# Two residual blocks on one core: the spatial gating unit computes v's columns before u's, and its layer norm and heads' mixing are issued among the large products

## What is computed

```python
def sgu_mixer(h, w_in, ln_g, ln_b, w_s, b_s, w_out):
    z = jax.nn.gelu(h @ w_in, approximate=False)
    u, v = jnp.split(z, 2, axis=-1)
    v = layernorm(v, ln_g, ln_b)
    v = v.reshape(B_, nc, SGU_CHUNK, SGU_HEADS, SGU_HEAD_DIM)
    ws = jnp.where(mask[None], w_s, 0)
    mixed = jnp.einsum('hts,bnshc->bnthc', ws, v) + b_s.T[None, None, :, :, None]
    gated = u * mixed.reshape(B_, S_, SGU_WIDTH)
    return gated @ w_out
```

## Time and profile before

| | |
|---|---|
| median of 3 runs | 2000.14 us |
| lowest, highest | 1999.51, 2003.49 us |
| the profiled execution, its time | 2002.35 us |
| its span in the profile | 2000.9 us |
| PE busy | 1825.2 us, 91% |
| DVE busy | 1052.0 us, 53% |
| ACT busy | 645.0 us, 32% |
| granted TensorE clock, mean over the span | 0.941 |

### The profile page before, as it was taken

One profiled execution on the slowest core, in us unless ns is written; L12 is line 12 of the kernel. 1 busy time (PEld: TensorE's weight loads), 2 busy tenths in 40 slices (PEclk: granted clock), 3 DMA queues, 4 the chain that ended last, 5 costly groups with the idle time before them and its releaser, 6 DMA issues.

```text
span 2000.9 us, 21459 instructions
## 1 busy us (share of the span) xinstructions
PE 1825.2 (91%) x8828; PEld 1473.2 (74%) x8828; DVE 1052.0 (53%) x1336; ACT 645.0 (32%) x796; POOL 82.5 (4%) x87
## 2 busy tenths in 40 slices
PE   4659999999896899999999989976599999999997
PEld 2238888888685688888886868855388888888885
DVE  4874675477426544234356574444565642456533
ACT  2123312322322243123244523332244431344412
POOL 2400010000000000000000101000000000000000
PEclk8769999999897899999998989987699999999997
DMA  9713474366230232323322240002123323232321
GB/s 356 275 64 105 143 236 151 102 209 222 74 105 9 76 105 87 104 88 102 105 90 69 85 100 4 4 1 66 40 85 105 100 90 105 84 105 91 100 84 42
DMA packets 124000, 208.55 MB, mean 104 GB/s; under 512 B 13965, under 2 KB 48421, under 8 KB 123904
## 3 DMA queue, kind: packets, MB, share of 16 engines
q1 hardware_dynamic: 115424, 174.94, 26.7%
q0 software_dynamic: 7808, 29.43, 4.4%
q10 hardware_dynamic: 672, 2.82, 0.4%
HBM read 204.01 MB, written 4.73 MB: 104 GB/s over the span
## 4 chain that ended last, share of the span: by engine, by line
PE 85%; DVE 10%; ACT 2%; DMA 1%; issue 1%; SPq 1%; DVEq 0%; ACTq 0%
PE bank L531 73%; DVE ada_acc L1643 2%; DMA ada_ring<-in_ada_w 1%; PE bank L878 1%; PE bank L547 1%; PE bank L861 1%; PE bank L841 1%; SPq L476 1%; PE bank L542 1%; DVE gT L1969 1%; DVE outer L1967 0%; PE bank L923 0%; PE bank L673 0%; PE bank L902 0%; PE bank L950 0%
## 5 line engine op out<-in xcount | busy, mean ns | idle before, releaser
L1568 DVE TENSOR_TENSOR w_lo<-raw,w_hi 128x2048 fp32r<-128x2048 f32 x138 | 316.2, 2292 | 533.0 <-ACT w_hi L1140 533.0
L1140 ACT ACTIVATE w_hi<-raw 128x2048 fp32r<-128x2048 f32 x138 | 263.8, 1912 | 632.7 <-PE bank L531 609.8
L531 PE MATMUL bank<-u_hi,w_hi 128*128 128x512 f32 x768 | 300.6, 391 | 0.8 <-DVE conv L2225 0.8
L531 PE MATMUL bank<-h_hi,w_hi 128*128 128x512 f32 x736 | 292.8, 398 | 7.9 <-DVE h_lo L1615 7.7
L531 PE MATMUL bank<-u_hi,w_lo 128*128 128x512 f32 x768 | 299.1, 389 | 0.0
L531 PE MATMUL bank<-u_lo,w_hi 128*128 128x512 f32 x768 | 298.9, 389 | 0.0
L531 PE MATMUL bank<-h_lo,w_hi 128*128 128x512 f32 x736 | 289.4, 393 | 0.0
L531 PE MATMUL bank<-h_hi,w_lo 128*128 128x512 f32 x736 | 289.2, 393 | 0.0
L531 PE MATMUL bank<-f_hi,w_hi 128*128 128x512 f32 x512 | 200.4, 391 | 2.4 <-DVE f_lo L1618 2.4
L531 PE MATMUL bank<-f_lo,w_hi 128*128 128x512 f32 x512 | 199.9, 391 | 0.0
L531 PE MATMUL bank<-f_hi,w_lo 128*128 128x512 f32 x512 | 199.8, 390 | 0.0
(11 more groups left out here) (351 smaller groups left out, 2040.3 us busy)
## 6 DMA issues: line engine op xcount, KB each, us to landing
raw<-in_mlp_w SPq DMA_DIRECT2D x128, 512.0 KB, 4.6
raw<-in_w_ffn_up SPq DMA_DIRECT2D x64, 512.0 KB, 4.4
ada_ring<-in_ada_w POOLq DMA_DIRECT2D x24, 1024.0 KB, 5.8
ada_ring<-in_ada_w SPq DMA_DIRECT2D x9, 2048.0 KB, 13.9
raw<-in_w_ffn_down SPq DMA_DIRECT2D x32, 512.0 KB, 4.4
raw<-in_w_in SPq DMA_DIRECT2D x20, 512.0 KB, 4.4
raw<-in_sgu_w_in SPq DMA_DIRECT2D x16, 512.0 KB, 4.9
x_rows<-in_ada_w SPq DMA_DIRECT2D x3, 2048.0 KB, 11.8
```

The source lines that it names most:

```text
L531: mm = te.matmul(bank[:, n], a, b, start=first and k == 0 and j == 0, stop=last and k == 3 and j == 2)
L1140: se.activation(m.ring(s)[0], m.raw[:, slot], ACT.Copy).then_inc(sem("hi_made"), 1)
L1568: ve.tensor_tensor(lo, m.raw[:, slot], hi.bitcast(F32), ALU.subtract).then_inc(sem("lo_made"), 1)
```

## The change

The same products and the same small operations are issued in another order.

- The weight slabs of `sgu_in` come in the order of column groups 2, 3, 0, 1. Groups 0 and 1 now make v, groups 2 and 3 make u.
- PE issues the turning and the bias spread after slab 34, the column sums inside slab 35 (after its second tile), heads 0 to 3 after the four tiles of slab 38, heads 4 and 5 after slab 39, and heads 6 and 7 after the first two tiles of slab 40. `sgu_out`'s first slab is no longer in k-outer order.
- ACT copies the bias during group 1, takes the root between slab 37's rounding and slab 38's, and rounds heads 0 to 3 ahead of slab 40's rounding, 4 and 5 ahead of slab 41's, 6 and 7 behind it.
- DVE masks between the `w_lo` of slabs 35 and 36, folds the bias, takes statistics and normalises between those of 36 and 37, and gates heads 0 to 3 behind slab 39's, 4 and 5 behind slab 40's, 6 and 7 behind slab 41's.

The core of the diff:

```diff
-    out = mlp(0) + linear(t["sgu_w_in"], 2, range(4)) + linear(t["sgu_w_out"], 2, range(2)) + mlp(1)
+    out = mlp(0) + linear(t["sgu_w_in"], 2, (2, 3, 0, 1)) + linear(t["sgu_w_out"], 2, range(2)) + mlp(1)
...
+    def spatial_weights(k, n):
+        if (k, n) == (0, 3):
+            te.wait_ge(sem("ws_in"), 32)
+            te.wait_ge(sem("scaled"), 8 * NORMED[NORM_MIX1] + 8)
+            for hh in range(DT):
+                mm = te.transpose(bank[:, 4 + hh // 4, P * (hh % 4):P * (hh % 4) + P], m.ws[:, hh], ident)
...
+        elif (k, n) == (1, 1):
+            te.wait_ge(sem("ws_masked"), MILESTONE["ws_masked"])
+            te.wait_ge(sem("bs_copied"), MILESTONE["bs_copied"])
...
+    def first_heads(k, n):
+        if k == 0:
+            mix_head(n)
+
+    def last_heads(k, n):
+        if k == 0 and n < 2:
+            mix_head(6 + n)
...
-    two_slabs("sgu_out", 2, m.g_hi, m.g_lo, gated, k_outer=True)
+    two_slabs("sgu_in", 0, m.h_hi, m.h_lo, lambda k: normed(NORM_MIX1, k), weights_stationary=False, k_outer=True)
+    two_slabs("sgu_in", 1, m.h_hi, m.h_lo, weights_stationary=False, beside=spatial_weights)
+    two_slabs("sgu_in", 2, m.h_hi, m.h_lo)
+    two_slabs("sgu_in", 3, m.h_hi, m.h_lo, beside=first_heads)
+    mix_head(4)
+    mix_head(5)
+    two_slabs("sgu_out", 0, m.g_hi, m.g_lo, gated, beside=last_heads)
+    two_slabs("sgu_out", 1, m.g_hi, m.g_lo)
...
         split_to(s + 1)
+        if g == 1:
+            se.wait_ge(sem("bs_spread"), MILESTONE["bs_spread"])
+            se.activation(m.bs[:, :], bank[:, 6:8].rearrange("p b n -> p (b n)"), ACT.Copy).then_inc(sem("bs_copied"), 1)
+        if g == 2:
+            se.wait_ge(sem("v_stats"), 4)
+            se.activation(m.mv[:, :, 1:2], m.mv[:, :, 1:2], ACT.Sqrt, bias=m.eps[:, 1:2]).then_inc(sem("v_rooted"), 1)
+        if g == 3:
+            gated_hi(range(4))
         split_to(s + 2)
...
+    gated_hi(range(4, 6))
+    split_to(SLABS["sgu_out"] + 1)
+    gated_hi(range(6, 8))
...
+    first = SLABS["sgu_in"]
+    split_to(first + 3)
     ve.wait_ge(sem("ws_turned"), MILESTONE["ws_turned"])
...
+    split_to(first + 4)
...
+    v_stats()
+    v_normed()
     ve.wait_ge(own.sem, bs_ready)
...
+    split_to(first + 7)
+    gate(range(4))
+    split_to(first + 8)
+    gate(range(4, 6))
+    split_to(first + 9)
+    gate(range(6, 8))
```

More of the change, by code:

```diff
@@ L685, in tensor_program @@
     norm_spread(NORM_MIX1)
[L688 to L716, removed]
+    def two_slabs(name, g, hi, lo, before_k=None, weights_stationary=True, k_outer=False, beside=None):
+        group, s = GROUPS[name] + g, SLABS[name] + 2 * g
+        for k in range(2):
+            def before_n(n):
+                emptied(group - 1, n)
+            def wait_k(kk):
+                before_k(4 * k + kk)
+            def after_n(n):
+                if beside:
+                    beside(k, n)
+            slab(s + k, group, hi[:, 4 * k:4 * k + 4], lo[:, 4 * k:4 * k + 4], k == 0, k == 1,
+                 wait_k if before_k else None, before_n, weights_stationary, k_outer and k == 0, after_n)
+            after_n(3)
@@ new lines, in spatial_weights @@
+    def spatial_weights(k, n):
[4 more added lines that the diff above has]
+                mm = te.transpose(bank[:, 4 + hh // 4, P * (hh % 4):P * (hh % 4) + P], m.ws[:, hh], ident)
+            mm.then_inc(sem("ws_turned"), 1)
+            for q in range(2):
+                mm = te.matmul(bank[:, 6 + q], ones[0:1, :], m.bs_row[0:1, 512 * q:512 * q + 512], start=True, stop=True)
+            mm.then_inc(sem("bs_spread"), 1)
+        elif (k, n) == (1, 1):
+            te.wait_ge(sem("ws_masked"), MILESTONE["ws_masked"])
+            te.wait_ge(sem("bs_copied"), MILESTONE["bs_copied"])
+            for q in range(2):
+                mm = te.matmul(bank[:, 6 + q], ones[:, :], m.wsT[:, 4 * q:4 * q + 4].rearrange("p h t -> p (h t)"), start=True, stop=True)
+            mm.then_inc(sem("ws_summed"), 1)
@@ L717, in tensor_program, with mix_head @@
+    def mix_head(hh):
         if hh >= 2:
@@ L1265, in scalar_program, with gated_hi @@
     normalise_hi(NORM_MIX1, m.h_hi, lambda k: m.modv(1, 0, k))
+    def gated_hi(heads):
+        for hh in heads:
+            se.wait_ge(sem("gated"), hh + 1)
+            se.activation(m.g_hi[:, hh], m.u[:, hh], ACT.Copy).then_inc(sem("gated_hi"), 1)
     for g in range(4):
@@ L1271, in scalar_program @@
             full(s + 1, group, n)
-            place = m.u[:, 4 * g + n] if g < 2 else m.v[:, n, 512 * (g - 2):512 * (g - 2) + 512]
+            place = m.v[:, n, 512 * g:512 * g + 512] if g < 2 else m.u[:, 4 * (g - 2) + n]
             se.activation(place, bank[:, n], ACT.Gelu).then_inc(sem("act_emptied"), 1)
[L1274 to L1280, removed]
+    gated_hi(range(4, 6))
+    split_to(SLABS["sgu_out"] + 1)
+    gated_hi(range(6, 8))
     for g in range(2):
@@ L1811, in vector_program, with v_stats, v_normed, gate @@
     normalise_lo(NORM_MIX1, m.xT, m.h_lo, m.h_hi, lambda k: m.gain[:, 16 + k:17 + k], lambda k: m.modv(1, 0, k))
-    for g in range(4):
-        split_to(SLABS["sgu_in"] + 2 * g + 2)
+    def v_stats():
+        for n in range(4):
+            for q in range(2):
+                emptied(GROUPS["sgu_in"] + q, n)
+                st = own.on(ve.bn_stats(m.stats[:, n, q], m.v[:, n, 512 * q:512 * q + 512]))
+            ve.wait_ge(own.sem, st)
+            ve.bn_aggr(m.mv[:, n], m.stats[:, n]).then_inc(sem("v_stats"), 1)
+    def v_normed():
+        ve.wait_ge(sem("v_rooted"), MILESTONE["v_rooted"])
+        ve.wait_ge(sem("v_stats"), 4)
+        n = own.on(ve.reciprocal(m.mv[:, :, 1:2], m.mv[:, :, 1:2]))
+        ve.wait_ge(own.sem, n)
+        for n in range(4):
+            ve.tensor_scalar(m.v[:, n], m.v[:, n], m.mv[:, n, 0:1], m.mv[:, n, 1:2], ALU.subtract, ALU.mult).then_inc(sem("v_normed"), 1)
+    def gate(heads):
+        for hh in heads:
+            ve.wait_ge(sem("heads_full"), hh + 1)
+            ve.scalar_tensor_tensor(out=m.tmp[:, hh % 2].rearrange("p (n t) -> p n t", n=4),
+                                    in0=bank[:, 4 + hh % 2].rearrange("p (n t) -> p n t", n=4), scalar=m.col("sgu_ln_g", hh),
+                                    in1=m.bs[:, P * hh:P * hh + P].unsqueeze(1).broadcast_to([P, 4, P]),
+                                    op0=ALU.mult, op1=ALU.add).then_inc(sem("heads_mixed"), 1)
+            ve.wait_ge(sem("heads_mixed"), hh + 1)
+            emptied(GROUPS["sgu_in"] + 2 + hh // 4, hh % 4)
+            ve.tensor_tensor(m.u[:, hh], m.u[:, hh], m.tmp[:, hh % 2], ALU.mult).then_inc(sem("gated"), 1)
+            ve.wait_ge(sem("gated"), hh + 1)
+            ve.wait_ge(sem("gated_hi"), hh + 1)
+            ve.tensor_tensor(m.g_lo[:, hh], m.u[:, hh], m.g_hi[:, hh].bitcast(F32), ALU.subtract).then_inc(sem("gated_lo"), 1)
+    first = SLABS["sgu_in"]
+    split_to(first + 3)
     ve.wait_ge(sem("ws_turned"), MILESTONE["ws_turned"])
@@ L1823, in vector_program @@
     bs_ready = n
[L1824 to L1835, removed]
-    ve.wait_ge(own.sem, bs_ready)
[L1837 to L1847, removed]
+    v_stats()
+    v_normed()
+    ve.wait_ge(own.sem, bs_ready)
+    split_to(first + 7)
[4 more added lines that the diff above has]
+    gate(range(6, 8))
     for g in range(2):
```

## The result

| | before | changed |
|---|---|---|
| median of 5 runs | 1999.58 us | 1977.61 us |
| lowest, highest | 1999.46, 2003.49 | 1975.86, 1982.51 |
| the profiled execution | 2002.35 | 1977.91 |
| its span | 2000.9 | 1976.5 |

The ratio of changed to before is 0.9887, with a 95% interval of 0.9872 to 0.9901. The kernel is 22.0 us faster by the medians and 24.4 us by the spans of the two profiled executions. The forecast was 1975.8 us, 24.3 us faster; the measured median lies 1.8 us above it, within the range of 1973 to 1982.5.

A forecast was written before the change was run, and what follows sets the result against it. PE bounds the kernel, busy 91% of the span; the SGU stretch offers 37.71 us, less 13.4 us of small matmuls among the products, a gain of 24.3: 2000.14 - 24.3 = 1975.8 us, range 1973 to 1982.5.

The forecast's parts named there:

- What was to win: Between sgu_in and sgu_out: 36.64 us of PE mostly waiting plus 1.07 us of slow start, 37.71 us.
- sums: Column sums on PE, 4 pieces moved among the products: 1.92 us at full clock.
- heads: Eight heads' matmuls on PE among the products: 8 x 0.97 = 7.76 us.
- changes: 18 changes between kinds of matmul on PE: 0.05 us each, 0.9 in all, with ends of 0 and 2.2.
- rival 2: Heads wait for one another through DVE's strict queue; slab 41 comes 11 us late, 1984 to 1992 us; chance 0.06.
- the 0.12 outside the range: Chance of a time outside 1973 to 1982.5 us, which the prediction gave to the two rarer rivals.
- At slab 37 I had 1.1 us of cover: Behind the layer norm: slab ready at 9.8 us after slab 35's end, due at 10.9.
- At slab 41 I had 0.7: Behind the gates: head 7 gated at 41.7 us after slab 38's start, wanted at 42.4; the thinnest place.
- Rival 1: Rounding or gates come late at slab 37, 41 or both, paid once: 1977 to 1983 us, middle 1979; chance 0.18.
- a rare rival that costs slabs or nothing: Short matmuls among products, slabs 38 to 40, lower PE's clock, 10.88 us per slab; chance 0.02 slower, 0.02 partly.
- no wait is met only at the end of the stage: Denies the rival that one such wait brings the serial stretch back, time as before within 4 us; chance 0.02.
- The slower case: From 2.3 slabs at half clock, of six from 38 to 43, the change is slower; all six give 2041; chance 0.02.

The follow-up runs named there:

- the delay: Two unneeded DVE additions in the changed kernel, ahead of the normalising (slab 37: 1979.08 us) or of the gates of heads 6 and 7 (slab 41: 1983.75 us).
- the order alone: The changed kernel with v's columns still computed first, but all small work issued behind the last slab as before: 2001.14 us, ratio 0.9998 to before.
- The doubled heads: The changed kernel with each head's four matmuls issued twice in the same place, the second time over the first result: 1986.71 us, ratio 0.9928 to before.

## Why the prediction was right

**The terms.** What was to win, 37.71 us, was read correctly from the one execution of before. The small matmuls in the stream cost 0.87 + 1.91 + 1.72 + 8 x 0.89 = 11.6 us by the chain, and 0.45 us for all the changes between them (110.0 less nine slabs of 10.88 and the 11.6), in all 12.1; I had said 13.4. Three terms were a little too large: sums 1.92 for 1.72, heads 7.76 for 7.12 (the weight loads of a head span 0.97 us, but the next product starts 0.89 us after the head's first matmul), changes 0.9 for 0.45. With the measured terms, 37.7 - 12.1 = 25.6 us, which is the stretch's gain. Two slips in the text of the prediction moved nothing: rival 2 has PE wait 0.6 us for each head in one clause and 1.4 in the next, and the 0.12 outside the range belongs to three rivals, not two.

**The covers.** At slab 37 I had 1.1 us of cover; the trace has 1.4, and the delay found 1.25. At slab 41 I had 0.7; the trace has 0.8, and the delay found 0.65. Both experiments found the edge where it was said to be. Rival 1 did not happen, but it would need only a microsecond to.

**The table load.** The row says 1.28 us and the root begins 0.01 us behind it, so a switch of set takes 1.29 us here, not the 2.66 that the Trainium skill gives in "ScalarE: Activation LUTs", section "What ACT_TABLE_LOAD costs"; the measurement decides. With 1.37 us more the cover at slab 37 would have been gone. The load for Gelu, at 577.16 us, is followed by its Gelu after 0.02 us too. All three loads of the stage, two more than before, were hidden: PE waited for none.

**From the stage to the median.** Of the 25.6 us in the stretch, 24.4 appear in the spans. The difference lies ahead of the change: the spread of the norm in front of the SGU came at 506.71 us in the profiled execution of before and at 508.55 in this one, because the mean's matmuls took 1.35 us in the one and 1.87 in the other, and small differences ahead of them add up. Behind the stage the two executions are alike within 0.4 us. So it is partly luck that these 24.4 us meet the forecast's 24.3, and the end of `sgu_out`, 658.54 us, its 658.4: the stretch gave 1.3 us more than forecast, and a late start took it back.

The medians differ by 22.0, 2.3 less than forecast. The interval allows 19.8 to 25.6 us, so that is no more than the executions vary, and its cause is not shown. Two things point the same way. The median of before that I subtracted from was 0.56 us above that of five executions. And the 37.71 us hold 1.25 us of column sums at half clock, which the order alone did not have behind the same instructions, so an ordinary execution of before may have less to win than the profiled one. The fall of the clock behind the bias spread, 1.6 us, came in one of seven and is too rare to move a median. I had put the insertions' clock at 1.00 from one window behind `sgu_in`, and held the fall for a rare rival that costs slabs or nothing. In the change it was shorter than that, eight products, and in both executions with the spread repeated it came.

**The rivals.** The heads did not wait for one another (gates 2.85 us apart where they follow directly), and no wait is met only at the end of the stage: PE waits for no other engine in it from 545 to 660 us. The slower case needed 2.3 slabs at half clock; the most that was seen in this stage of the change is eight products.

## What to carry to other kernels

A serial stretch of small operations between two dense ones is worth its whole length less what its matmuls cost in the stream: 37.7 us less 12.1 here. Write down for each moved step the next weight slab that queues behind it on the same engine, and its cover; two covers of about 1 us bounded this design, and 4.0 us of lateness at the second cost 6.4, since PE started again at half clock. Look at the granted clock behind matmuls with one row or with two columns even where PE never stops. Loading the bias already spread took 2.2 us out of this stage, but the time did not show it, so time such a change for itself before you keep it.

## What the runs showed of the hardware that was not expected

- The granted clock fell to half while PE was issuing without a gap: at 0.50 during the repeated one-row matmuls of 553 to 556 us, for eight products behind a single pair of them in one of seven executions, and behind 32 pieces of 128 rows by two columns in three of thirteen, where it cost 3.2 us. The doubled heads, 128 rows by 128 columns, kept 1.00.
- The Trainium skill, "TensorE: Matmul & The Clock Gate", Part 1, lays the clock to how busy PE has been. The clock at 0.50 behind waits of 1.84 and 7.33 us agrees. The fall during the repeated spread is not explained by it, if busy is what the profile calls so: the rows have PE busy for 3.00 of 3.00 us there.
- PE's wait of 1.50 us at slab 37 cost 1.8 us in all and left the clock at full speed; two waits of 1.84 and 1.68 us at slab 41 made it 4.0 us late and cost 2.4 us more, and the clock stood at 0.50 already between them, in 629 to 630 us.
- A switch of activation table took 1.28 us and the next instruction followed in 0.01 to 0.02 us.
